# Encoder layer on eight cores: weights cast as they are first loaded, norm weights on rows, Fourier folds after the projection

## The reference

```python
h = rmsnorm(x, g_mix)
q, k, v, f = split(h @ w_in, [1024, 2048, 3072])        # 1024, 1024, 1024, 512 columns
q = rope(rmsnorm(q per 64-wide map, g_q)); k = rope(rmsnorm(k per map, g_k))   # 16 maps
a = softmax(q0 k0^T / 8) - lam * softmax(q1 k1^T / 8)   # 8 heads, two maps each, 2048 x 2048
o = rmsnorm(a @ v, g_sub) * 0.2
attn_out = o @ w_attn_br
fr = real(fft2(f in 4 groups of 128 channels, over rows and channels, ortho))
four_out = fr @ w_four_br
gates = sigmoid(h @ w_gate + b_gate)                    # two gates of 1024
x = x + (gates0 * attn_out + gates1 * four_out) @ w_out
h2 = rmsnorm(x, g_mlp)
y = x + square(relu(h2 @ w_up)) @ w_down                # 4096 wide
```

## Time and profile before

| | us |
|---|---|
| median of 3 runs | 4971.37 (4956.44 to 5246.41) |
| the profiled execution | 4961.58 |
| its span, core 1 (the slowest) | 4959.7 |
| spans of the other cores | 4917.0 to 4954.5 |
| PE busy | 4145.0 (84%) |
| ScalarE / VectorE / Pool busy | 2963.6 / 2666.3 / 504.4 |

### The profile page before, as it was taken

One profiled execution on the slowest core, in us unless ns is written; L12 is line 12 of the kernel. 1 busy time (PEld: TensorE's weight loads), 2 busy tenths in 40 slices (PEclk: granted clock), 3 DMA queues, 4 the chain that ended last, 5 costly groups with the idle time before them and its releaser, 6 DMA issues.

```text
span 4959.7 us, 50893 instructions; the slowest of 8 cores (4917.0 to 4959.7 us)
## 1 busy us (share of the span) xinstructions
PE 4145.0 (84%) x18084; PEld 1560.4 (31%) x18084; DVE 2666.3 (54%) x4525; ACT 2963.6 (60%) x5369; POOL 504.4 (10%) x430
## 2 busy tenths in 40 slices
PE   5765665778999878999787989998788799899999
PEld 2221111223343323333223333332223244344444
DVE  1666655446634646677773366667775433233233
ACT  4566667768744668888775455787777621421521
POOL 0541000000002510000100143000100000100100
PEclk9976776889999999999788999999779899999999
DMA  9359999877773367777878623778778833633632
GB/s 249 130 157 246 245 245 245 187 181 176 147 204 116 118 160 183 157 167 156 203 151 233 195 84 101 146 156 202 164 159 208 149 88 120 197 99 123 200 102 77
DMA packets 1114430, 821.79 MB, mean 166 GB/s; under 512 B 917696, under 2 KB 1005120, under 8 KB 1093440
## 3 DMA queue, kind: packets, MB, share of 16 engines
q1 hardware_dynamic: 1046352, 515.48, 47.1%
q10 hardware_dynamic: 67824, 303.06, 18.8%
HBM read 476.57 MB, written 115.34 MB: 119 GB/s over the span
## 4 chain that ended last, share of the span: by engine, by line
PE 46%; ACT 21%; DMA 16%; DVE 9%; issue 5%; POOL 2%; ACTq 1%; SPq 1%; DVEq 0%; POOLq 0%
PE pall L471 46%; ACT sb_ov L484 20%; DMA sb_ov<-sb_ov 13%; DVE sb_ov L495 4%; DVE sb_ov L492 3%; POOL sb_ov L492 2%; DVE sb_ov L499 1%; DMA fr_d<-sb_ov 1%; ACTq L514 1%; ACT sb_sm L484 1%; DVE sb_sm L495 0%; DMA wb_mix<-sb_ov 0%; SPq L517 0%; DMA q_d<-sb_ov 0%; DMA sb_ov<-x 0%
## 5 line engine op out<-in xcount | busy, mean ns | idle before, releaser
L471 PE MATMUL pall<-sb_ov 128*128 128x512 bf16 (+1 forms) x15552 | 3612.2, 395 | 621.9 <-ACT sb_ov L484 519.6
L484 ACT ACTIVATE sb_ov<-pall 128x1024 bf16<-128x1024 f32 (+2 forms) x2379 | 2036.0, 869 | 1319.6 <-PE pall L471 1116.7
L471 PEld LDWEIGHTS pall<-sb_ov 128*128 128x128 bf16 (+1 forms) x15552 | 1334.5, 98 | 2796.4 <-ACT sb_ov L484 910.7
L492 DVE TENSOR_TENSOR sb_ov<-pall,sb_ov 128x512 f32<-128x512 f32 (+1 forms) x912 | 619.9, 690 | 608.1 <-PE pall L471 443.2
L492 POOL TENSOR_TENSOR sb_ov<-sb_ov 128x512 f32<-128x512 bf16 (+3 forms) x396 | 488.9, 1256 | 4199.1 <-DVE sb_ov L492 2142.6
L495 DVE SCALAR_TENSOR_TENSOR sb_ov<-sb_ov,sb_sm 128x2048 bf16<-128x2048 bf16 x384 | 906.7, 2361 | 13.5
L492 DVE TENSOR_TENSOR sb_ov<-sb_ov 128x512 bf16<-128x512 bf16 (+4 forms) x614 | 402.9, 660 | 534.6 <-ACT sb_ov L484 481.0
L484 ACT ACTIVATE sb_ov<-sb_ov 128x512 f32<-128x512 f32 (+3 forms) x628 | 514.8, 825 | 276.1 <-DMA sb_ov<-sb_ov 120.3
L471 PE MATMUL pall<-sb_ov,sb_vall 128*128 128x512 bf16 x1536 | 408.2, 427 | 59.1 <-DMA sb_ov<-sb_ov 59.0
L484 ACT ACTIVATE sb_ov<-pall,sb_sm 128x512 f32<-128x512 f32 x384 | 262.4, 686 | 278.9 <-PE pall L471 136.1
L471 PE MATMUL pall<-sb_ov,sb_cmat 128*128 128x128 bf16 (+2 forms) x924 | 207.9, 323 | 129.9 <-DVE sb_ov L495 79.8
(11 more groups left out here) (33 smaller groups left out, 269.4 us busy)
## 6 DMA issues: line engine op xcount, KB each, us to landing
sb_ov<-wb_mix ACTq DMA_DIRECT2D x96, 896.0 KB, 5.7
sb_ov<-x SPq DMA_DIRECT2D x96, 512.0 KB, 8.7
sb_ov<-k_d SPq DMA_DIRECT2D x96, 512.0 KB, 5.2
sb_ov<-wb_up ACTq DMA_DIRECT2D x48, 1024.0 KB, 5.3
sb_ov<-wb_down ACTq DMA_DIRECT2D x48, 1024.0 KB, 5.4
sb_ov<-hT_d SPq DMA_DIRECT2D x48, 512.0 KB, 4.8
sb_ov<-wb_out ACTq DMA_DIRECT2D x24, 1024.0 KB, 5.7
y<-sb_ov SPq DMA_DIRECT2D x48, 512.0 KB, 3.8
```

What stands on the lines that cost most here:

```text
L471: P.op("pe", lambda e: e.matmul(out, lhsT=lhsT, rhs=rhs, start=start, stop=stop), reads, writes, us)
L484: P.op("act", lambda e: e.activation(out=out, in_=in_, func=func, **kw), reads, writes, us)
L492: P.op(eng, lambda e: e.tensor_tensor(out=out, in0=in0, in1=in1, op=op), reads, writes, vus(eng, n, mode))
```

## The change

The conversion streams go. A weight is now a `Tile` with its parts; the first time that a ring feeds it, its parts are loaded by DMAs that cast f32 to bf16, issued on Pool's queue (one for each part of 4 row blocks by 512 or 256 columns; gates and branch weights are cut by pairs of column tiles), and the tile is then stored to its own bf16 copy from SP's queue, after a planned slack of 6 us. Later feeds read the copy on ScalarE's queue as before. `xstream` has such a ring for every sequence (four tiles of 512 KB; V is cut in four tiles, K and Q in eight of 256 columns). There are 20 casting DMAs in the first projection and 66 in the first block of `ystream`. The scratch for Pool's DMA descriptors grows from 1024 to 2048. `ystream` starts at `pdone` of sequence 0 and waits for no conversion.

The norm weights are no longer folded into weights: they are loaded as rows on all partitions (`gains`), and the norm of x and the second norm multiply by them in the same pass (`STT` for `TS1`).

`fourier` loads hT in four loads of 512 rows, projects the rows as they are (and reversed copies of half of them, made on ScalarE and Pool by `turned`), and adds and subtracts the projected 128x512 results as they leave PSUM; the middle row is projected apart. The number of projection matmuls is 128 as before, and 16 for the middle row. The chunk's inputs are fetched ahead of `fourier` rather than after it.

```diff
-            self.clock[e] = st + 0.06
+            self.clock[e] = st + (1.2 if e == "pool" else 0.06)
...
-        for eng in ("sp", "act"):
+        for eng in ("sp", "act", "pool"):
...
-                    if t > now or any(self._clash(self.pend[j], p) for j in range(i)):
+                    if t + p.slack > now or any(self._clash(self.pend[j], p) for j in range(i)):
...
-SCR = 1024
+SCR = 2048
...
-    wb_v = dscr("wb_v", [2, 128, 4096], BF16)
...
-    wb_down = dscr("wb_down", [8, 128, 4096], BF16)
...
-        def wcast(job, lo, bo):
...
-                    ACT(o, a, AF.Copy, cf + ["vecs"], cb, 512, scale=None if gain is None else gain[:, k:k + 1])
...
-                    TS1(o, a, gain[:, k:k + 1], ALU.mult, cf + ["vecs"], cb, 512)
...
-            DMAL(dst, v, ("ws", bo), [("wb16", bo, k) for k in range(kk)] + cells(bo, n), [key], kk * 128)
...
+        class Tile:
+            def __init__(self, name, n, parts):
+
+                self.n, self.parts, self.key = n, parts, ("wb", name)
+                self.copy = None
+                self.name = name
+
+        def whole(name, src, k, w, cuts):
+
+            kk = k // cuts
+            return Tile(name, k * w, [(i * kk * w, src[:, i * kk:(i + 1) * kk], (kk, w)) for i in range(cuts)])
...
+                if not self.todo:
+                    return
+                t = self.todo.pop(0)
+                lo = self.lo + i * self.size
+                if isinstance(t, Tile) and t.copy is None:
+                    for j, (o, src, (kk, w)) in enumerate(t.parts):
+                        m = kk * w
+                        DMAL(ovb(lo + o, m).rearrange("p (k n) -> p k n", k=kk), src, (self.name, i, "c", j), [], cells(lo + o, m), m / 2, q="pool")
+                    t.copy = dscr("wb_" + t.name, [128, t.n], BF16)
+                    DMAL(t.copy, ovb(lo, t.n), (self.name, i, "s"), cells(lo, t.n), [t.key], t.n / 4, slack=6.0)
+                else:
+                    src, keys = (t.copy, [t.key]) if isinstance(t, Tile) else (t, [])
+                    n = t.n if isinstance(t, Tile) else 4096
+                    DMAL(ovb(lo, n), src, (self.name, i, 0), keys, cells(lo, n), n / 4, q="act")
+                self.queue.append(lo)
 
...
+        wx = [Tile("v%d%d" % (i, h), 2048, [(0, w_in_r[:, 4 * h:4 * h + 4, 2048 + i * 512:2048 + (i + 1) * 512], (4, 512))])
+              for i in range(2) for h in range(2)]
+        wx += [whole("%s%d" % (nm, i), w_in_r[:, :, c0 + i * 256:c0 + (i + 1) * 256], 8, 256, 2)
+               for nm, c0 in (("k", 1024), ("q", 0)) for i in range(4)]
...
+                DMAL(ovf(glo, 1024), gains_d[0], "gx", [], cells(glo, 2048), 512)
...
-                    TS1(h, x, sm[:, 12 + i:13 + i], ALU.mult, cx + [key], chb, 1024)
+                    STT(h, x, sm[:, 12 + i:13 + i], ovf(glo, 1024), ALU.mult, ALU.mult, cx + cells(glo, 2048) + [key], chb, 1024)
...
+                ring = Ring("xw", XW_ * KB, 2048, 4, list(wx))
...
+                los = [ring.get() for _ in range(4)]
...
+            tf = whole("f", w_in_r[:, :, 3072:3584], 8, 512, 2)
+            tmix = []
+            for j in range(4):
+                c = slice(j * 256, (j + 1) * 256)
+                tmix.append(Tile("g%d" % j, 4096, [(gi * 2048 + h * 1024, w_gate_r[:, 4 * h:4 * h + 4, gi * 1024 + j * 256:gi * 1024 + (j + 1) * 256], (4, 256))
+                                                   for gi in range(2) for h in range(2)]))
+                tmix.append(Tile("a%d" % j, 3072, [(h * 1024, w_attn_r[:, 4 * h:4 * h + 4, c], (4, 256)) for h in range(2)] +
+                                 [(2048, w_four_r[:, :, c], (4, 256))]))
+            tout = [whole("o%d" % i, w_out_r[:, :, i * 512:(i + 1) * 512], 8, 512, 2) for i in range(2)]
+            tup = [whole("u%d" % n, w_up_r[:, :, n * 512:(n + 1) * 512], 8, 512, 2) for n in range(8)]
+            tdn = [whole("d%d" % n, w_down_r[:, (n // 2) * 8:(n // 2) * 8 + 8, (n % 2) * 512:(n % 2 + 1) * 512], 8, 512, 2) for n in range(8)]
...
-            yield Need(flags=[("pdone", 0), "small"])
-            ring = Ring("yw", YW0 * KB, NYW, plan_f() + plan_blk())
+            yield Need(flags=[("pdone", 0)])
+            ring = Ring("yw", YW0 * KB, 4096, NYW, plan_f() + plan_blk())
...
+            prefetch(0, 0)
-            yield Need(flags=["converted"])
-            prefetch(0, 0)
...
-                        TS1(hb, xt, sm[:, 50 + n:51 + n], ALU.mult, cx + [key], chb, 1024)
+                        STT(hb, xt, sm[:, 50 + n:51 + n], ovf(glo, 1024), ALU.mult, ALU.mult, cx + cells(glo, 2048) + [key], chb, 1024)
...
+                        prefetch(*nxt)
                         yield from fourier(s + 1, ring, Y)
-                        prefetch(*nxt)
...
-            def hload(k):
...
-                TT(ft[:, 1:N2], h[:, 1:N2], h[:, SEQ - 1:N2:-1], op, ch, cft, N2, eng=eng)
...
-                    fold(hq.pop(0), k, half)
...
+            hv = ovb(Y(F_H), 16384).rearrange("p (k t) -> p k t", k=8)
+            ch = [[x for k in range(8) for x in cells(Y(F_H) + k * 2048 + c * 512, 512)] for c in range(NTC)]
+            for c in range(NTC):
+                DMAL(hv[:, :, c * 512:(c + 1) * 512], hT_d[s][:, :, c * 512:(c + 1) * 512], ("fh", c), [("hT_d", s, c)], ch[c], 1024)
...
+            def turned(tt, i, eng):
...
+                if eng == "act":
+                    ACT(o, src, AF.Copy, c, cz, 1024)
+                else:
+                    P.op(eng, lambda e: e.tensor_copy(out=o, in_=src), c, cz, vus(eng, 1024))
+            yield Need(keys=ch[3])
+            turned(0, 3, "pool")
+            yield Need(keys=ch[2])
+            P.op("pool", lambda e: e.memset(view(z2)[:, :, 0:1], 0.0), [], cells(z2, 1024), 0.2)
+            P.op("pool", lambda e: e.tensor_copy(out=view(z2)[:, :, 1:128], in_=hv[:, :, N2 + 1:N2 + 128]), ch[2], cells(z2, 1024), 2.3)
+            yield Need(keys=ch[1])
+            turned(0, 1, "act")
...
+            for tt in range(4):
+                for n, (i0, i1) in enumerate(((0, 3), (1, 2))):
+                    bb = []
+                    for i in (i0, i1):
+                        v, cv = seg(tt, i)
+                        yield Need(keys=cv + cwf, pool=POOLY, nbanks=1)
+                        b = P.alloc(POOLY)
+                        bb.append(b)
+                        for k in range(8):
+                            MM(bank(b), v[:, k, :], ovb(wf + k * 512, 512), k == 0, k == 7, cv + cwf, [bk(b)])
+                        if i % 2 and tt + 1 < 4:
+                            turned(tt + 1, i, "act")
+
+                    e0, e1 = [Y(F_E + 4 * n + 2 * x) for x in range(2)]
+                    CP(ovf(e1, 512), bank(bb[0]), [bk(bb[0])], cells(e1, 1024), 512, eng="act")
+                    P.free(bb[0])
+                    TT(ovf(e0, 512), ovf(e1, 512), bank(bb[1]), ALU.add, [bk(bb[1])] + cells(e1, 1024), cells(e0, 1024), 512)
+                    TT(ovf(e1, 512), ovf(e1, 512), bank(bb[1]), ALU.subtract, [bk(bb[1])] + cells(e1, 1024), cells(e1, 1024), 512)
+                    P.free(bb[1])
+                for x, (o, op) in enumerate(((0, ALU.add), (0, ALU.subtract), (1, ALU.subtract), (1, ALU.add))):
+                    d, a0, a1 = Y(F_C + 4 * x + tt), Y(F_E + 2 * o), Y(F_E + 4 + 2 * o)
+                    TT(ovb(d, 512), ovf(a0, 512), ovf(a1, 512), op, cells(a0, 1024) + cells(a1, 1024), cells(d, 512), 512,
+                       eng="pool" if x % 2 else "dve")
+
...
+            for x in range(2):
+                yield Need(keys=cmid + cwf, pool=POOLY, nbanks=1)
+                b = P.alloc(POOLY)
+                for k in range(8):
+                    MM(pall[0:1, b, :], mid[:, x, k:k + 1], ovb(wf + k * 512, 512), k == 0, k == 7, cmid + cwf, [bk(b)])
...
-        P.merge([conv1(), xstream(), avstream(), conv2(), ystream()])
+            P.flags[("fr", s)] = True
```

More of the change, by code:

```diff
@@ L165, in _dma, with later @@
         return ins
-    def later(self, eng, fn, slot, reads=(), writes=(), us=3.0, flags=()):
-        p = Later(eng, fn, slot, tuple(reads), tuple(writes), us, tuple(flags))
+    def later(self, eng, fn, slot, reads=(), writes=(), us=3.0, flags=(), slack=0.0):
+        p = Later(eng, fn, slot, tuple(reads), tuple(writes), us, tuple(flags), slack)
         if all(f in self.flags for f in flags):
@@ L511, in DMA, with DMAL @@
             P.dma(q, lambda e: e.dma_start(out=out, in_=in_), slot, reads, writes, us=kb / 200.0)
-        def DMAL(out, in_, slot, reads, writes, kb, q="sp", flags=()):
-            P.later(q, lambda e: e.dma_start(out=out, in_=in_), slot, reads, writes, kb / 200.0, flags)
+        def DMAL(out, in_, slot, reads, writes, kb, q="sp", flags=(), slack=0.0):
+            P.later(q, lambda e: e.dma_start(out=out, in_=in_), slot, reads, writes, kb / 200.0, flags, slack)
         def DMAT(out, in_, slot, reads, writes, kb):
@@ L635, in split @@
-        def split(job):
-            src, kk, gain, dst, view, key, layout = job
-            if kk == 4:
```

(29 more changed lines are left out.)

355 lines of the change are left out of this document (118 added, 237 removed).

## The result

The changed kernel takes 0.9643 of the time of the kernel before (95% interval 0.9602 to 0.9685); a second comparison on another chip gave 0.9639 (0.9600 to 0.9678). Its profiled execution has 4784 us against 4962, a span of 4782.7 against 4959.7. It is faster, as forecast, but by 177 us where I had forecast 380: 4580 was too low, and 4784 lies above my range of 4410 to 4760. Some executions of either kernel run 3 to 7% longer, with the cores of one die or of both at a lower granted clock; the ratios compare the others alone.

The account below looks back on a forecast made before the run. PE is the bound in the tail and starves in three kinds of places elsewhere, some 820 us lost. Gains 25 + 262 - 50 + 148 - 5 = 380 us off 4959.7 give 4580 us, range 4410 to 4760.

Parts of the forecast that it names:

- Conversion gone: First sequence's attention: without the conversion, its matmuls from 334 to 890 run at the following stretch's rate; gain 262 us.
- The 1111 matmuls of 334 to 890 take 1111 / 3.78 = 294 us: First sequence's attention: matmuls costed at the rate just after the conversion, 3.78 a microsecond; gain 262 us.
- output blocks out of work while attention runs alone: Sign of being wrong: the output stream lacks work while attention runs alone at 2.9 matmuls a microsecond.
- Crowding: First sequence's attention: f32 reads and stored copies bring the DMA share to 0.98, with transposes behind stores on SP; loss 50 us.
- Fourier: Fourier stages of sequences 1 and 2: four loads and folding after projection replace the chain of folds; gain 148 us.
- at 4.27 they take 352, at 3.78 398: Fourier stages of sequences 1 and 2: 1504 matmuls that took 523 us run at good stretches' rates; gain 125 to 171.
- Start: First projection: shorter waits for cast weights gain 40 us, Pool's issuing of casts costs 15; net gain 25 us.
- norm weights: 96 norm passes take two tensors, 0.45 us more each on VectorE; mostly hidden, loss 5 us.
- Pool as the bound: Rival: first loads pass Pool's one in-order queue, held issues delay all behind; slower, 5060 us at 21.7 us a cast; chance 0.06.
- A0 saturates: Rival, first sequence's attention: DMA engines saturate, transposes stay at 8.3 us, 136 instead of 50 us lost; 4666 us; chance 0.15.
- the Fourier stage stays long: Rival, Fourier stages: attention's pace, not the folds, stretched them, so the 148 us gain goes; 4728 us; chance 0.12.
- the last output rows of the first block, forecast at 1416: First block's end: its last output rows, stored at 1653.38 before, would be stored 237 us earlier.

Follow-up runs that it names:

- first run: Changed kernel, but the first sequence's output blocks read the hidden rows in place of the attention's result, so they wait for no head; 0.9527 of the kernel before.

## Why the prediction was half right

*Conversion gone (forecast 262, less 50 of crowding; 132 measured).* The step that failed is "The 1111 matmuls of 334 to 890 take 1111 / 3.78 = 294 us". It priced matmuls at the rate of a neighbouring stretch without asking which of them could be there: from 890 to 1387 the output stream had all eight heads of its two chunks before it, from 334 it has the Fourier stage and one chunk for the time of 16 heads. The stretch from 321 to 1292 reached 3.30 matmuls a microsecond. I had named this sign ("output blocks out of work while attention runs alone") without giving it a chance. Supplying the work gains 58 us.

*Crowding (forecast 50; 78 by the run without casts).* The sign was right, the size low, and the reason partly wrong. I had a DMA share of 0.98; it is 0.86 over the stretch, against 1.05 and 0.75 in its two parts before, and 1.12 in the worst 100 us. I counted stores and reads alike; without the stores nothing changed that can be measured, so the casts carry it. The feared stores on SP, waiting for their cast, did not matter. Transposes landed in a median of 4.9 us, against 8.5, and ScalarE still waited 92.5 us for them.

*Fourier (forecast 148; 78 in the stages, 54 to 70 in the end).* The chain of folds is gone as described, and the second sequence's stage runs at 3.73 a microsecond once it runs, near the 3.78 I had as the lower bound. But the stages take 226 and 155 us, where I had named about 100 as the sign of being right and over 200 as that of being wrong. The step that failed is "at 4.27 they take 352, at 3.78 398": it left out that the stage's loads of 4 MB meet 4 MB of stored rows on full DMA engines, which loses 49 and 32 us at the two starts. That wait is not the whole reason: with the loads brought forward the start is full and the time the same, since the rest of the attention loses 83 us in place of 41. Part of the gain was also given back in the first sequence. With the old stage its Fourier results are stored by 562, head 8 at 548 and the last rows of the first block at 1394; with the new one at 507, 571 and 1405 (core 1 of both). So there the earlier Fourier stage only waits longer for head 8.

*Start (forecast 25; 18) and norm weights (5; nothing to measure).* The first held, and nothing speaks against the second. A pass with norm weights takes 1285 ns, against my 1218 by the earlier trace rows.

*The rivals.* Pool as the bound did not come: the last of the 66 casts was issued at 1313, some 15.5 us a cast, where that rival needed 21.7. The price that the Trainium skill gives for a transfer caught by VectorE ("SBUF — State Buffer", section "A bandwidth-pool intuition that's wrong (but worth ruling out)", some 3.1 us) shows in no issue: the 86 casts took 0.74 to 0.93 us each on Pool. Those issued beside VectorE's work in the first projection have a mean of 0.77 us:

```profile
L507 POOL DMA_DIRECT2D sb_ov<-w_in x22 | 16.9, 769 | 98.9 <-PE pall L464 80.7 <-issue 17.3 <-POOLq L396 0.9
```

Of the rival "A0 saturates" (86 us on top of the forecast) a third came true, of "the Fourier stage stays long" (148) some 94, and the missing supply, 58 us, was no rival at all. Each alone lies inside the range, and their sum just reaches its end: 28 + 94 + 58 = 180, which gives 4760. The other 24 of the 204 us between 4580 and 4784 are not assigned. The two large terms could fall short together because both were priced by a borrowed rate.

One date misled me: the last output rows of the first block, forecast at 1416, were stored at 1405. The output stream did gain the 248 us, but attention gained 95 (its last head at 1292, where 237 less would be 1150). I had counted the gain of one stream as that of the kernel.

What stays open: why the casts delay the transposes and as many stored bytes do not, and what holds a transpose some 20 us next to a burst in another queue. No complete version here is faster than the changed kernel beyond the uncertainty.

## What to carry to other kernels

A freed stretch runs at its neighbour's rate only if the same work is there to run: list what each stream can do at that time, and what it waits for, before multiplying matmuls by a rate. When DMA engines come to 1.0 in bursts, shortening one stage can move the stall to the next burst, as with the early loads here; judge an edit by the lost matmul time of the whole span, not by its own stage. Two streams that share an engine trade time: with more work for the output stream (first run) the first sequence's attention ended at 1375 in place of 1292, and the kernel was still 58 us faster.

## What the runs showed of the hardware

- Filling TensorE raised its granted clock from 0.62 and 0.69 to 0.98 and 0.91, and the heads came no faster: 29 us each (four from 719 to 835, and from 712 to 829). Eight half steps of ScalarE's passes and hand-overs make 22.6 us of that; the rest is not taken apart here.
- A MB of bf16 that is cast from f32 on its way takes 7.4 us of all DMA engines, a plain one 3.4. 27 MB of stores more or less made no measurable difference.
- A single transpose was held up to 15.5 us on SP in the changed kernel, and up to 26.5 and 24.7 us when the bulk loads stood in another queue; most take some 2 us.
